# First MLP's second projection: six of its sixteen weight blocks multiplied in rounded products, their low halves made by adding DMAs, and the near sets of the S5 layer issued by GpSimd

## What is computed

```python
# layer 0 of the first block: MLP (w_fc1: 1024 x 4096, w_fc2: 4096 x 1024)
h = _rmsnorm(x, norm_g[layer, 1]) * (1.0 + scale_f) + shift_f
x = x + gate_f * (jnp.square(jax.nn.relu(h @ w_fc1[layer])) @ w_fc2[layer])
# layer 1: a bidirectional S5 mixer; its matrices (powers of the state's factor, kernels of a
# chunk) depend on parameters alone
mix = _mixer_s5(h, s5_lam_re[i], s5_lam_im[i], s5_log_step[i], s5_b_re[i], ...)
```

## Time and profile before

| | us |
|---|---|
| median of 3 runs | 1171.31 |
| lowest and highest | 1170.61, 1175.93 |
| profiled execution, its span | 1171.0 |
| `fc2_0` with what runs beside it | 306.7 to 443.7 |

### The profile page before, as it was taken

The page is one execution under the profiler, slowest core; times in us unless marked ns, Lnnn a source line. Parts: engine busy times, 40 slices in busy tenths (PEclk is TensorE's granted clock), DMA queues, the critical chain, the costliest instruction groups (busy, mean ns, idle before and its releaser), DMA issues.

```text
span 1171.0 us, 22089 instructions
## 1 busy us (share of the span) xinstructions
PE 1112.6 (95%) x9466; PEld 995.9 (85%) x9466; DVE 816.0 (70%) x1390; ACT 557.7 (48%) x876; POOL 44.6 (4%) x71
## 2 busy tenths in 40 slices
PE   6899898999999997879999999999999999999998
PEld 4778686988888885469999999999988899988898
DVE  1599466877578674875666654478899966659955
ACT  3224633445111124554555543356568846467944
POOL 0010001000000000000000000000000000042000
PEclk8999999999999998999999999989989999999999
DMA  9887688899848957865355555525433345343342
GB/s 369 356 280 269 250 323 315 305 339 328 335 182 258 342 186 165 323 245 184 140 184 182 183 189 185 187 81 180 145 109 114 130 153 177 131 153 117 108 145 72
DMA packets 38290, 246.46 MB, mean 210 GB/s; under 512 B 4400, under 2 KB 5584, under 8 KB 9648
## 3 DMA queue, kind: packets, MB, share of 16 engines
q1 hardware_dynamic: 29072, 182.36, 45.7%
q0 software_dynamic: 6240, 43.94, 10.0%
q10 hardware_dynamic: 2880, 18.74, 3.9%
HBM read 225.24 MB, written 19.79 MB: 209 GB/s over the span
## 4 chain that ended last, share of the span: by engine, by line
PE 78%; DVE 10%; DMA 5%; ACT 5%; issue 2%; SPq 0%; ACTq 0%; DVEq 0%
PE ps L1452 16%; PE ps L1454 15%; PE ps L1456 15%; PE ps L1459 10%; PE ps L1555 4%; DMA ca_dram<-more 2%; PE ps L1648 1%; PE ps L1528 1%; PE ps L2083 1%; PE ps L1601 1%; PE ps L1539 1%; PE ps L1534 1%; DMA more<-in_ada_w 1%; DVE ring_rounded L2229 1%; DMA ada_more<-in_ada_w 1%
## 5 line engine op out<-in xcount | busy, mean ns | idle before, releaser
L1452 PE MATMUL ps<-sq_rounded,w_high_rounded 128*128 128x256 f32 x1184 | 341.6, 288 | 2.5 <-DVE mixT_rounded L2236 1.3
L1456 PE MATMUL ps<-sq_rounded,ring_rounded 128*128 128x256 f32 x1184 | 336.2, 284 | 0.0
L2229 DVE TENSOR_TENSOR ring_rounded<-ring,w_high_rounded 128x1024 fp32r<-128x1024 f32 x220 | 260.6, 1226 | 92.1 <-ACT w_high_rounded L844 91.8
L1454 PE MATMUL ps<-hT_rounded,w_high_rounded 128*128 128x256 f32 x992 | 282.1, 284 | 0.0
L844 ACT ACTIVATE w_high_rounded<-ring 128x1024 fp32r<-128x1024 f32 x220 | 219.8, 1049 | 67.0 <-PE ps L1456 66.3
L1452 PEld LDWEIGHTS ps<-sq_rounded,w_high_rounded 128*128 128x128 f32 x1184 | 228.5, 193 | 11.0 <-issue 6.7
L1456 PEld LDWEIGHTS ps<-sq_rounded,ring_rounded 128*128 128x128 f32 x1184 | 228.6, 193 | 0.0
L1454 PEld LDWEIGHTS ps<-hT_rounded,w_high_rounded 128*128 128x128 f32 x992 | 191.8, 193 | 0.1
L1452 PE MATMUL ps<-more_rounded,w_high_rounded 128*128 128x256 f32 x448 | 127.4, 284 | 0.4 <-issue 0.3
L1456 PE MATMUL ps<-more_rounded,ring_rounded 128*128 128x256 f32 x448 | 126.8, 283 | 0.0
L1459 PE MATMUL ps<-big,ring 128*128 128x256 f32 x544 | 121.0, 381 | 0.0
(11 more groups left out here) (426 smaller groups left out, 1640.3 us busy)
## 6 DMA issues: line engine op xcount, KB each, us to landing
ring<-in_blocks SPq DMA_DIRECT2D x139, 1024.0 KB, 4.9
ada_w<-in_ada_w POOLq DMA_DIRECT2D x27, 1024.0 KB, 7.7
ada_more<-in_ada_w POOLq DMA_DIRECT2D x13, 1024.0 KB, 7.6
we_dram<-we_t ACTq DMA_DIRECT2D x8, 1024.0 KB, 8.3
ca_dram<-more ACTq DMA_DIRECT2D x8, 1024.0 KB, 11.9
ring<-we_dram SPq DMA_DIRECT2D x8, 1024.0 KB, 5.5
ring<-ca_dram SPq DMA_DIRECT2D x8, 1024.0 KB, 6.8
big<-in_ada_w SPq DMA_DIRECT2D x4, 1024.0 KB, 10.9
```

What stands on the lines that cost most here:

```text
L1452: nc.tensor.matmul(out, high[:, k, columns], x_high, start=start, stop=False, skip_group_check=True)
L1454: nc.tensor.matmul(out, high[:, k, columns], x_low, start=False, stop=False, skip_group_check=True)
L1456: last = nc.tensor.matmul(out, low[:, k, columns], x_high, start=False, stop=stop, skip_group_check=True)
L2229: nc.vector.tensor_tensor(rounded(w), w, w_high[:, c % 2, ks], ALU.subtract)\
```

## The change

- In `fc2_0` the k-blocks are taken in the order of `FC2_ORDER`. Blocks 5, 7, 8, 10, 12 and 13 (`FC2_SPLIT`: units 1 to 3, k-blocks 0 and 1) become split blocks; the other ten stay plain.
- For these six, ScalarE makes two passes over the whole block: the rounded block into `w_high`, and minus the rounded block into the ring slot. Then GpSimd issues a DMA of the block from DRAM that adds to the slot (`accum_op`), which leaves the low half. VectorE's `lower_to` leaves them out. TensorE does the 32 matmuls with the high half first and waits for the adding DMA before the 16 with the low half.
- `hid` tiles 0 to 15 are rounded by ScalarE (eight `round_tiles`, ahead of `store_kernels(1)`), into `sq` and `hT`, and lowered in place by VectorE (eight `lower_tiles` in turn 4, behind block 3).
- ScalarE's passes stand in its loop of turns: block 5 ahead of `store_outputs(3)`, blocks 7, 8, 10, 12 and 13 behind `store_outputs` of turns 3 to 7. A wait for block 12 stands ahead of the norm's squares.
- All four near sets are issued by GpSimd: 0 and 1 once blocks 12 and 13 are done, 2 and 3 once the stage's last block is done and the set two before has landed.
- Three pairs or triples of small transfers share a semaphore (`lam_here`, `small_here`).

```diff
+FC2_ORDER = ((0, 1, 2, 3), (2, 0, 3, 1), (0, 2, 1, 3), (0, 1, 2, 3))
+FC2_SPLIT = tuple(4 * n + i for n in range(1, 4) for i in range(4) if FC2_ORDER[n][i] < 2)
+FC2_ROUND_BEHIND = {3: 7, 4: 8, 5: 10, 6: 12, 7: 13}
+LOW_BY_DMA = {"fc2_0": (5, 7, 8, 10, 12, 13)}
...
         @block.sync
-                if b in NEAR_AT:
-                    load_near(NEAR_AT.index(b))
...
-                    if nb == RING - 1:
-                        load_near(2)
-                        load_near(3)
...
         @block.gpsimd
+            def add_low(name, j):
+
+                b = first_block[name] + j
+                pool.wait_ge(w_high_ready, 2 * split_place[b] + 2)
+                pool.dma_start(rounded(ring[:, b % RING]).rearrange("p a b -> p (a b)"), dram["blocks"][laid_out[b]],
+                               accum_op=ALU.add).then_inc(w_low_added[split_place[b] % 2], 16)
...
+            for j in FC2_SPLIT:
+                if j in LOW_BY_DMA["fc2_0"]:
+                    add_low("fc2_0", j)
+
+            for n in range(4):
+                pool.wait_ge(k_stored, 16 * (n + 1))
+                if n < 2:
+                    pool.wait_ge(blocks_done, first_block["fc2_0"] + FC2_SPLIT[n - 2] + 1)
+                else:
+                    pool.wait_ge(blocks_done, first_block["s5_in"])
+                    pool.wait_ge(near_here[n - 2], 16 * L)
+                for j in range(L):
+                    pool.dma_start(s5_near[n][GC * j:GC * j + GC],
...
         @block.scalar, round_to
+                    if b in low_added:
+                        nc.scalar.activation(w_high[:, c % 2], ring[:, b % RING], ACT.Copy).then_inc(w_high_ready, 1)
+                        nc.scalar.activation(rounded(ring[:, b % RING]), ring[:, b % RING], ACT.Copy, scale=-1.0)\
+                            .then_inc(w_high_ready, 1)
...
+            for t in range(8):
+                act.wait_ge(hid_ready, t + 1)
+                round_tiles(hid0_high(2 * t, 2), hid[:, 2 * t:2 * t + 2])
             store_kernels(1)
             store_outputs(2)
             for m in range(3, 8):
...
                 store_weights(m)
+                if m == 3:
+                    round_to(first_block["fc2_0"] + FC2_SPLIT[0] + 1)
                 store_kernels(m - 1)
                 store_outputs(m)
+                if m in FC2_ROUND_BEHIND:
+                    round_to(first_block["fc2_0"] + FC2_ROUND_BEHIND[m] + 1)
...
+            act.wait_ge(blocks_done, first_block["fc2_0"] + FC2_SPLIT[-2] + 1)
             norm_stats(2, 2)
...
         @block.tensor, block_products
+                if b in low_added:
+                    pe.wait_ge(w_high_ready, 2 * split_place[b] + 1)
+                    first = places[0][4]
+                    for k, out, columns, x, start, stop in places:
+                        if arrived and columns.start == 0:
+                            arrived(k)
+                        for part in x:
+                            nc.tensor.matmul(out, high[:, k, columns], part, start=first, stop=False,
+                                             skip_group_check=True)
+                            first = False
+                    pe.wait_ge(w_low_added[split_place[b] % 2], 16 * low_added[b])
+                    for k, out, columns, x, start, stop in places:
+                        last = nc.tensor.matmul(out, low[:, k, columns], x[0], start=False, stop=stop,
+                                                skip_group_check=True)
...
         @block.vector
             for m in range(3, 8):
                 s5_weights(m)
+                if m == 4:
+                    dve.wait_ge(blocks_done, first_block["fc2_0"] + 4)
+                    for t in range(8):
+                        lower_tiles("fc2_0", t, hid[:, 2 * t:2 * t + 2], hid0_high(2 * t, 2))
                 s5_outputs(m)
```

More of the change, by code:

```diff
@@ L171, in weight_plan @@
     phase("fc1_0", [("fc1_0", 0, n) for n in range(16)])
-    phase("fc2_0", [("fc2_0", k, n) for n in range(4) for k in range(4)])
+    phase("fc2_0", [("fc2_0", k, n) for n in range(4) for k in FC2_ORDER[n]])
     phase("s5_in", [("s5_in", 0, n) for n in range(8)])
@@ L215, in split_plan @@
 def split_plan(plan, first_block):
-    order, place, low = [], {}, {}
+    order, place, low, added = [], {}, {}, {}
     starts = sorted((b, name) for name, b in first_block.items())
@@ L223, in split_plan @@
         for b in range(start, end) if name in SPLIT_LO else ():
-            if b - start not in {"w_in": W_IN_SPLIT, "w_out": W_OUT_SPLIT}.get(name, range(end - start)):
+            if b - start not in {"w_in": W_IN_SPLIT, "w_out": W_OUT_SPLIT, "fc2_0": FC2_SPLIT}.get(name, range(end - start)):
                 continue
@@ L227, in split_plan @@
             order.append(b)
+            if b - start in LOW_BY_DMA.get(name, ()):
+                added[b] = 1 + sum(place[a] % 2 == place[b] % 2 for a in added)
+                low[b] = 0
+                continue
             counts[SPLIT_LO[name]] += 1
             low[b] = counts[SPLIT_LO[name]]
-    return order, place, low
+    return order, place, low, added
 def program(nc, dram, out):
     plan, first_block = weight_plan()
-    split_order, split_place, split_low = split_plan(plan, first_block)
+    split_order, split_place, split_low, low_added = split_plan(plan, first_block)
     laid_out = {b: i for i, b in enumerate(from_inputs(plan))}
-    NEAR_AT = (first_block["fc2_0"] + 10, first_block["fc2_0"] + 11)
     ctx = ExitStack()
@@ L341, in program @@
         w_low_vector = sem("w_low_vector")
+        w_low_added = [sem(f"w_low_added{i}") for i in range(2)]
         a_high = sem("a_high")
@@ L1441, in block_products @@
                     pe.wait_ge(w_here[b % RING], here[b])
+                if b in low_added:
[12 more added lines that the diff above has]
+                                                skip_group_check=True)
                 waited = 0
-                for k, out, columns, x, start, stop in places:
+                for k, out, columns, x, start, stop in places if b not in low_added else ():
                     if split and k // 4 == waited:
@@ L1837, in after_block, with hid_arrived, hid_low_arrived, hid_tile @@
                     s5_kernels(S5_KERNEL_AT.index(16 + j))
-            for n in range(4):
-                project_deep("fc2_0", n, 4, (hid,), lambda k: pe.wait_ge(hid_ready, k // 2 + 1) if k % 2 == 0 else None,
-                             after_block)
+            def hid_arrived(t):
+                if t % 2 == 0:
+                    pe.wait_ge(hid_ready, t // 2 + 1)
+            def hid_low_arrived(t):
+                if t < 2 * KB and t % 2 == 0:
+                    pe.wait_ge(a_low, SET_BASE["fc2_0"] + t // 2 + 1)
+            def hid_tile(t):
+                if t < 2 * KB:
+                    return rounded(hid0_high(t, 1)[:, 0]), rounded(hid[:, t])
+                return hid[:, t]
+            project_deep("fc2_0", 0, 4, lambda t: hid[:, t], hid_arrived, after_block, FC2_ORDER[0])
+            for n in range(1, 4):
+                project_deep("fc2_0", n, 4, hid_tile, hid_low_arrived if n == 1 else None, after_block, FC2_ORDER[n])
             norm_stats(2)
```

66 lines of the change are left out of this document (31 added, 35 removed).

## The result

| | kernel before | changed kernel |
|---|---|---|
| median of the runs | 1171.5 us | 1182.1 us (1175.5 to 1184.1) |
| profiled span | 1171.0 us | 1180.4 us |
| `fc2_0`: first fp32 matmul | 306.7 us | 310.6 us |
| from there to the norm's first matmul | 136.9 us | 145.4 us |
| norm to the first of `chunk_inputs(0)` | 13.3 us | 13.4 us |

The change is slower: 1.0062 of the time before (95% interval 1.0042 to 1.0083; the two medians alone make 1.0090); in a second comparison 1.0037 (1.0017 to 1.0056). It was to be 0.6% faster. The profiled executions differ by +9.4 us: +3.9 ahead of the stage, +8.5 in the stage, -3.1 in the S5 entry.

The account below looks back on a forecast made before the run. The prediction saw two equal bounds in the stage of `fc2_0`, TensorE and the S5 preparation. From 1171.3 us it took -4.5 in the stage and -2.3 behind it: 1164.5 us, range 1161 to 1174.

Parts of the forecast that it names:

- Part 3: Stores of `ca_dram` that hold VectorE: 8 us each (bounds 6.2 and 15.2), hidden; adds land in 10 us, engine share 0.77.
- the sum: Stage `fc2_0`: kernel matmuls of turn 7 start at 409.2 instead of 413.99 us, -4.8, taken as -4.5 us.
- Part 4: ScalarE's queue: block 7's passes delay the copy for TensorE's third bank, costing 1 us; bounds 0 and 9.
- Part 5: The adds' deadlines: only block 13's is tight, 9 us for its add, a stall of 0 to 6 us.
- Part 1: TensorE in `fc2_0`: each of six rounded blocks takes 5.85 us instead of 6.97, 6.7 us saved, no clock term.
- Part 2: VectorE's eight lowerings take 5.5 us; `s5_outputs(4)` ends near 356.2 and `s5_outputs(7)` at 405.8 us.
- rival A: Slower: adding DMAs cost much engine time and VectorE waits for stores; about 1175 to 1185 us, chance 0.17.
- 3 us to spare: TensorE's own end in the stage, 436.3 us, was to leave 3 us before the norm for block 13's stall.
- Rival B: Block 13's add is late, 15.2 us; the stage gains 0.5 us, all near 1168.5 us, chance 0.13.
- Part 6: Near sets issued by GpSimd instead of SP, and merged semaphores: nothing waits for them, 0 us.
- Part 7: Code stall of TensorE behind the stage: near sets 2 and 3 issued earlier shorten it, -2.3 us; bounds -5.3 and +2.
- The bound of 0.5%: What a measurement of this kernel can tell from no change: about 0.5%, 5.9 us, so faster means below 1165.4 us.

Follow-up runs that it names:

- e3_both: Changed kernel with ScalarE's passes over block 13 ahead of turn 7's store and over block 7 behind turn 4's: 0.9959 of the kernel before, 1171.3 us.
- e5_both_plain: e3_both with the six adding DMAs made plain loads, so the low halves are not made: 0.9923 of the kernel before, 1163.2 us.
- e4_near_alone: Kernel before with only the near sets moved to GpSimd, 0 and 1 behind blocks 12 and 13, no block split: 0.9988, 1174.0 us.
- e6_both_gpsimd: e3_both with low halves by GpSimd subtractions instead of adding DMAs, one ScalarE pass a block: 1.0113 of the kernel before, 1189.5 us.
- e8_both_four: Against e3_both, four split blocks (8, 10, 12, 13) instead of six, VectorE's lowerings behind block 7 in turn 5: 1.0079 of the kernel before, 1182.9 us.
- e1: Changed kernel with ScalarE's passes over block 13 ahead of turn 7's store instead of behind it: 0.9996 of the kernel before, 1173.7 us.
- f1: e3_both with block 13's low half made by VectorE instead of an adding DMA: 1.0000 of the kernel before, 1174.6 us.
- f2_low7_13_vector: e3_both with the low halves of blocks 7 and 13 made by VectorE, four adds left: 0.9942 of the kernel before, 1168.3 us.
- f3: e3_both with the low halves of blocks 7, 12 and 13 made by VectorE, three adds left: 0.9962 of the kernel before, 1171.1 us.

## Why the prediction was wrong, step by step

Three steps failed: the price of an adding DMA (Part 3), and the two waits of TensorE that the sum put at 1 us and 0 (Parts 4 and 5). The two waits cost the stage 5.8 and 7.0 us, and 4.3 us of lower clock behind them; the price of the adds stands behind both.

- **Part 1** was right in its price: rounded blocks at full clock took 5.85 to 5.93 us (blocks 7, 8 and 10), 6.7 us for six. Its "no clock term" was not: the clock of before did not stay when TensorE stood. Its end in the stage was 136.5 us; less 6.7 and less the wait of 1.27, plus 5.8 and 7.0 of new waits and 4.3 of lower clock, makes 145.6 (145.4 measured).
- **Part 2** was right in its terms, but held only without waits: eight lowerings took 4.8 us (5.5 forecast), and `s5_outputs(4)` ended at 359.4, or 355.5 on the clock of before (356.2). The seventh ended 10.4 us late, at 420.1 - 3.9 = 416.2 instead of 405.8. VectorE's waits make up 11.1 us: 3.2 for TensorE's late banks and 7.9 for stores (2.62, 1.33, 0.78, 3.19).
- **Part 3** failed in the price of an add: it was given a landing time (10 us; 10.7 measured) but the engine time of a plain load: 5.2 us of all engines for each MB, not 3.0. The share of 0.77 was too low even at a load's price: `e3_both` has 0.91 in 340 to 360 us and 1.01 or more in each 20 us from there to 440, and `e5_both_plain`, without adds, is nearly as full. There the stores still took 7.5 us, close to the 8 forecast; with adds they took up to 12.5. So it is the price that failed, and a full engine by itself did not make a store late. This is the mechanism of rival A. It is seen unmixed in `e3_both` and `e5_both_plain`, where it costs 6.1 us of the stage.
- **Part 4** failed in size: block 7's load was taken as 6.5 us, with a bound of 9 us of stall; the load took 11.4 and TensorE stood 6.07. I had the wait, its place and the bound, and chose a load time near those of the kernel before (this load took 5.2 there) for a moment when an add had just been issued (343.81). The runs show that this add made the load late: issued at the end of block 3, it took 5.0 to 5.3 us in the five profiles that have no transfer of GpSimd there (the kernel before twice, `e4_near_alone`, `e6_both_gpsimd`, `e8_both_four`), 8.1 beside a plain load (`e5_both_plain`) and 9.3 to 11.4 in the eight with the add. The landing rows of this load, in the kernel before and in `e3_both`:

```profile
ring<-in_blocks SPq DMA_DIRECT2D x1, 1024.0 KB, 5.2
...
ring<-in_blocks SPq DMA_DIRECT2D x1, 1024.0 KB, 9.4
```

- **Part 5** failed twice: block 13's passes stand behind a store whose own start follows VectorE, so they came with VectorE's 10 us; and the add took 13.9 us. TensorE stood 6.99, outside 0 to 6. "3 us to spare" was then no cover. Rival B had the mechanism and too small a price: it left out the wait at turn 4's banks and the clock that falls with each idle.
- **Part 6** holds: nothing waited for the near sets, and `e4_near_alone` shows the move to be harmless; in itself it is worth nothing that the runs can tell (0.9988, and 0.9987 for the kernel before again).
- **Part 7** came near in its number (-3.1 for -2.3 forecast, in a second profile -1.0), but by luck: its mechanism was not there. Near sets 2 and 3 were to be issued 2.9 us ahead of the norm. As TensorE ended last, GpSimd issued them 0.7 us behind the norm's start (456.02), where SP had issued them level with it (443.72 and 443.67). GpSimd's order of time and then TensorE's:

```profile
456.73 8.09 POOL L817 DMA_DIRECT2D big<-k_dram  x16 [9.49 <-issue]
...
476.19 1.71 PE L1936 MATMUL ps<-ring,hT 128*32 128x256 f32 x13 [2.03 <-issue]
```

Yet the stall is 2.03 us, 3.00 in the second profile, and 2.74 in `e4_near_alone` (sets issued 0.1 us behind the norm), for 5.27 and 5.31 in the kernel before. So it came with the move to GpSimd's queue and not with a lead; why is open. Other runs do have the lead, since their TensorE ends early: in the six profiles in which set 2 is issued 1.0 to 3.6 us ahead of the norm (those of the runs `e1`, `e3`, `e5`, `f1`, `f2` and `f3`) this stall is gone; at 0.7 us (`e6_both_gpsimd`) it is 3.5. In `f2_low7_13_vector` (3.6 us) the entry takes 23.0 us instead of 30.5, more than the 4.5 that its stage gains. No run has the lead alone, so this too is an observation.
- **The sum** treated Parts 3, 4 and 5 as separate small risks. They are one: they go through the same engines, which the adds hold longer, and the last add's start hangs on the stores. In place of -4.5 us the stage lost 8.5.
- The bound of 0.5% held for what it was for: the start of the stage alone moved by 6 us from profile to profile.

## What to carry to other kernels

Price a DMA that accumulates at more than the engine time of a load (1.75 times here), and look where it meets the transfers that somebody waits for; where another engine has the time, try to make some of the low halves there. When a step is put into an in-order queue, ask what it waits for and who needs the instruction behind it: here moving two pairs of passes brought back all of the loss. A gain on one engine is worth nothing until the other chain of the same length is shorter too. And when a number comes out, check that its mechanism did.

## What the hardware showed unexpectedly

An idle of TensorE costs more than its length: after 6 to 7 us the clock was 0.55 and 0.57 over the next 5 to 7 us, and 2.6 and 1.7 us were lost. An adding DMA takes 1.75 times the engine time of a load. A GpSimd subtraction of 128x1024 takes 3 us beside VectorE's products and makes these 2.7 times as long. The DMA engines were as good as full with plain loads too (a share of 0.93 to 1.00), and the stores still landed in 7.5 us. And the moment at which this stage starts differs by up to 6 us between profiles, with granted clocks of 0.94 to 1.00 in 40 to 70 us.
